# Feed-forward entries with in-place rows and direct sums, head norms rebuilt, forgetting scores as two passes of split operands

## The chip, the core and the metric

The kernel runs on one core of one Trainium2 chip. The metric is the device time of one execution in microseconds (us). A core has TensorE (matrix products, PE in the profile), VectorE (DVE), ScalarE (ACT), GpSimd (POOL) and SyncE (SP), whose queue here issues every transfer. Each engine works through its own list in order. Engines wait for one another by semaphores.

## What is computed

One layer of 1024 tokens, width 1024, in float32: two gated feed-forward blocks of inner width 2816 with a mixer and a cross attention to a memory of 256 rows between them. Each part has a norm ahead of it and one behind it. The mixer has eight heads of forgetting attention (64 wide) and four heads of gated linear attention (GLA). The parts that the change touches:

```python
# forgetting attention, for head h; c is the running sum of log_f
s = einsum('bhqd,bhkd->bhqk', qf[:, :, q0:L], kf[:, :, :L])       # qf holds q * 64 ** -0.5
s = s + c[:, :, q0:L, None] - c[:, :, None, :L]
p = softmax(where(mask, s, -inf));  o = einsum('bhqk,bhkd->bhqd', p, vf)
# norms of the heads, gate of GLA, output projection
o_fox = head_rms_norm(o, g_fox_out)
o_gla = head_rms_norm(gla_chunked(gq, gk, gv, log_a), g_gla_out) * silu(r)
y = concatenate([o_fox, o_gla]) @ w_out
# feed-forward
y = (silu(h @ w_gate) * (h @ w_up)) @ w_down
```

## The kernel before

Everything is static: each engine's list is written out in the code, and semaphores with constant counts order the engines.

*Products.* Most products are made of split operands: a high part (float32r, a rounded float32) and a low part (the remainder), three products each (hi hi, hi lo, lo hi). ScalarE makes the high part with a copy, VectorE the low part with a subtraction. Scores and a few others take float32 directly.

*Feed-forward, first half (`ff_1`).* Gate and up blocks of 256 columns are formed by a Strassen scheme with seven products P1, P2, P6, P5, P7, P3, P4 in that order. Their operands from x are B11, B21, T2, T1, T3, B22, T4. T1 and T2 are sums over tiles of tokens (`sum_x`), T3 and T4 are sums on top of T2 (`sum_x_late`). The operands from the weights are four groups: 0 and 3 come from the raw weights (`w_raw`), 1 and 2 from sums (`w_sums`). `high_x`, `low_x`, `high_w` and `low_w` split them. `fork_off` is a ScalarE copy of a PSUM bank that lets the next product reuse it: P7 waits for the second, P3 for the third. P4 waits for two block sums of VectorE. In the first block (m = 0) the products wait also for the tiles of x.

*An entry* is what leads to that first block. Eight tiles of 128 tokens are squared (ScalarE), get a root (GpSimd), become rows (`make_row`, VectorE), are turned by eight 128x128 transpositions (`turn`, TensorE, line 1248) into two PSUM banks and copied to `h_all` (`keep_h`). At f = 0 the rows pass through two buffers (`h_rows[0]`); the last two loads of x wait for earlier rows. The up weights (m = 1) are loaded in `ff_loads`, only after all T3 and T4 sums, since T2 lies in the buffer of those weights. The second entry (f = 1) runs inside the output loop of the cross attention, and behind it.

*Forgetting attention (`attend_fox`, lines 1375 to 1399).* Pairs of heads p = 0 to 3, for each 16 steps a: head a // 8, query block b = a % 8. Step a of TensorE is the scores of a (width 128 (b + 1)), the transpositions of the exponentials of a - 1, and the product with v of a - 2. Between them VectorE takes the row maximum and ScalarE the exponential. A score is one float32 product over 66 rows: 64 of q and k, one that holds c and one that holds ones; c comes to these rows by way of DRAM (`c_rows`, `load_c`). Behind step 15 the next pair's q and k are projected (`project`, lines 1316 to 1318), and both halves of k must be kept (`keep_q`) before the next scores. The projections' weights have three buffer pairs (`wr`), and `high_s(n)` waits for the projection n - 3. Sets are numbered: S_Q + 2p and the next are q and k of a pair, GQ to GQ+3 are those of GLA, GV its values, GR its gate, OUT the output weights.

*Behind it* TensorE transposes `k_flat` (`turn_k`, line 1428), which ScalarE copies once it has split GV and GV+1, then projects GQ+2 and GQ+3.

*Output projection.* For each tile i of 128 tokens: `gla_out` (four heads into bank 2), squares on ScalarE, sums on VectorE, root on GpSimd (L714), two scalings on VectorE (L1985, L1988), the gains and the gate on GpSimd (L720, L723), then `turn_o` (line 1506), high and low part (L1046, L1995), and 48 products (`out_tile`). Behind a tile `square1`, `root1` and `scale_y` make the new x (L780, L627, L1720, L1724).

## Time and profile before

| what | us |
|---|---|
| median of 3 runs | 2424.4 |
| lowest, highest | 2418.94, 2438.99 |
| the profiled execution: its time | 2420.73 |
| the profiled execution: its span | 2418.9 |
| TensorE busy in the span | 2282.0 |
| VectorE, ScalarE, GpSimd busy | 1090.1, 776.5, 477.2 |

The span is from the first to the last instruction. L1278 is line 1278 of the kernel. A row of the order of time gives the start, the duration, engine, line, operation, out<-in, the shapes and how many are merged; in brackets stands how long the engine was idle before it and what released it. The releaser is inferred: where the named one had long been done, it was another. "issue" means that nothing in the profile explains the idle time. The ends of products are modelled, so starts are the better measure. The granted clock is TensorE's, 1.00 for full speed.

### The profile page before, as it was taken

The numbers are of one execution on the slowest core, as the hardware profiler recorded it, in microseconds if no ns is written. First come the engines' busy times: TensorE is split into PE (matmuls) and PEld (weight loads), VectorE is DVE, ScalarE is ACT, GpSimd is POOL, SyncE is SP. The second block draws the span as 40 slices with busy tenths as digits, with TensorE's granted clock in tenths as the row PEclk, the third lists the DMA queues.
The fourth block names the chain that finished last, engine by engine and source line by source line (L and its number), as shares of the span: only waits on it lengthen the run. The fifth ranks groups of instructions, "written<-read, shape, count | busy, mean of one in ns | idle before, by whom it ended". The sixth has DMA issues, their size and how long they took to land.

```text
span 2418.9 us, 27006 instructions
## 1 busy us (share of the span) xinstructions
PE 2282.0 (94%) x10640; PEld 1856.6 (77%) x10640; DVE 1090.1 (45%) x1332; ACT 776.5 (32%) x1218; POOL 477.2 (20%) x455
## 2 busy tenths in 40 slices
PE   4899999999999999999999899989699999999997
PEld 3688888878877777778777687758588888878886
DVE  6444444464455244452234443234744444445446
ACT  5333333331123423331222243333533333332113
POOL 1344434300011000000123300001134434320003
PEclk8999999999999999999998899989799999999999
DMA  2222222253332000001221152023122222233323
GB/s 96 87 79 91 93 70 87 70 174 97 114 102 83 26 19 19 19 27 53 76 82 53 44 183 79 18 70 93 64 70 87 87 88 88 70 130 123 107 93 122
DMA packets 104958, 195.45 MB, mean 81 GB/s; under 512 B 6993, under 2 KB 72546, under 8 KB 102018
## 3 DMA queue, kind: packets, MB, share of 16 engines
q1 hardware_dynamic: 104834, 193.73, 24.4%
q8 instruction: 86, 1.41, 0.2%
q14 instruction: 38, 0.31, 0.0%
HBM read 153.80 MB, written 39.91 MB: 80 GB/s over the span
## 4 chain that ended last, share of the span: by engine, by line
issue 46%; PE 44%; POOL 4%; DVE 2%; POOLq 2%; ACT 1%; DMA 1%; DVEq 0%; SPq 0%; ACTq 0%
PE ps L1278 10%; PE ps L1279 10%; PE ps L1280 10%; PE ps L1296 3%; PE ps L1297 3%; PE ps L1298 3%; PE ps L1316 1%; PE ps L1318 1%; PE ps L1317 1%; POOL rs L627 1%; POOL rs L634 1%; POOL o_rms L714 1%; POOLq L721 1%; POOLq L633 0%; DMA w_raw<-in_w_ff_up 0%
## 5 line engine op out<-in xcount | busy, mean ns | idle before, releaser
L1278 PE MATMUL ps<-xc,wg 128*128 128x512 f32 x1232 | 484.4, 393 | 40.2 <-ACT fork L831 13.4
L1279 PE MATMUL ps<-xc,wg 128*128 128x512 f32 x1232 | 483.6, 392 | 0.0
L1280 PE MATMUL ps<-xc,wg 128*128 128x512 f32 x1232 | 482.9, 392 | 0.0
L1278 PEld LDWEIGHTS ps<-xc,wg 128*128 128x128 f32 x1232 | 234.0, 190 | 91.0 <-issue 37.6
L1296 PE MATMUL ps<-d_w,d_hid 128*128 128x512 f32 x704 | 276.1, 392 | 6.7 <-DVE y L1821 6.7
L1297 PE MATMUL ps<-d_w,d_hid 128*128 128x512 f32 x704 | 275.1, 391 | 0.0
L1298 PE MATMUL ps<-d_w,d_hid 128*128 128x512 f32 x704 | 275.0, 391 | 0.0
L1280 PEld LDWEIGHTS ps<-xc,wg 128*128 128x128 f32 x1232 | 233.8, 190 | 49.0
L1279 PEld LDWEIGHTS ps<-xc,wg 128*128 128x128 f32 x1232 | 233.9, 190 | 48.6
L1788 DVE TENSOR_TENSOR wg<-w_sums,wg 128x1024 fp32r<-128x1024 f32 x88 | 123.4, 1402 | 196.8 <-ACT wg L825 196.8
L1824 DVE TENSOR_TENSOR y<-y,ps 128x1024 f32<-128x1024 f32 x88 | 107.4, 1220 | 216.2 <-PE ps L1298 216.2
L1296 PEld LDWEIGHTS ps<-d_w,d_hid 128*128 128x128 f32 x704 | 133.0, 189 | 35.6 <-issue 7.5
L1788 DVE TENSOR_TENSOR wg<-w_raw,wg 128x1024 fp32r<-128x1024 f32 x88 | 129.4, 1471 | 55.8 <-ACT wg L825 55.8
L1298 PEld LDWEIGHTS ps<-d_w,d_hid 128*128 128x128 f32 x704 | 132.8, 189 | 27.8
L1297 PEld LDWEIGHTS ps<-d_w,d_hid 128*128 128x128 f32 x704 | 133.0, 189 | 27.5
L831 ACT ACTIVATE fork<-ps 128x512 f32<-128x512 f32 x132 | 78.7, 597 | 228.1 <-PE ps L1280 228.1
L654 POOL TENSOR_TENSOR hid<-hid,up_sum 128x512 f32<-128x512 f32 x66 | 89.2, 1352 | 265.0 <-DVE up_sum L1801 265.0
L825 ACT ACTIVATE wg<-w_sums 128x1024 fp32r<-128x1024 f32 x88 | 93.0, 1057 | 112.0 <-PE ps L1280 110.4
L625 POOL TENSOR_SCALAR ms<-ss 128x1 f32<-128x1 f32 x32 | 7.1, 223 | 572.4 <-ACT junk L780 572.4
L853 ACT ACTIVATE d_hid<-raw 128x1024 fp32r<-128x1024 f32 x44 | 46.5, 1057 | 220.1 <-PE ps L1298 134.4
L825 ACT ACTIVATE wg<-w_raw 128x1024 fp32r<-128x1024 f32 x88 | 74.3, 844 | 128.7 <-PE ps L1280 120.5
L641 POOL TENSOR_TENSOR w_sums<-w_raw 128x512 f32<-128x512 f32 x42 | 73.8, 1757 | 197.5 <-DVE wg L1788 145.2
(263 smaller groups left out, 3834.2 us busy)
## 6 DMA issues: line engine op xcount, KB each, us to landing
w_raw<-in_w_ff_gate SPq DMA_DIRECT2D x22, 1024.0 KB, 6.6
w_raw<-in_w_ff_up SPq DMA_DIRECT2D x22, 1024.0 KB, 5.2
hid_dram<-hid SPq DMA_DIRECT2D x22, 1024.0 KB, 4.6
raw<-hid_dram SPq DMA_DIRECT2D x44, 512.0 KB, 3.7
raw<-in_w_ff_down SPq DMA_DIRECT2D x44, 512.0 KB, 3.6
raw<-in_w_mix_in SPq DMA_DIRECT2D x24, 512.0 KB, 3.8
x_row<-x_dram SPq DMA_DIRECT2D x24, 512.0 KB, 4.1
x_dram<-x_ring SPq DMA_DIRECT2D x16, 512.0 KB, 5.0
```

The lines of the kernel that those rows point to most:

```text
L641: gp.tensor_tensor(s[1], r[:, 0:4, 1, :], r[:, 4:8, 1, :], ALU.add).then_inc(w_summed, 1)
L654: gp.tensor_tensor(blk, blk, up_sum[:, j, :], ALU.mult).then_inc(hid_done, 1)
L825: sc.activation(group_dst(g, 0), group_src(m, g), ACT.Copy).then_inc(w_hi_done, 1)
L831: sc.activation(fork[:, j, :], ps[:, 3 * (m % 2) + (0, 0, 2)[j], :], ACT.Copy).then_inc(forked, 1)
L1278: mm(acc, hi, x_hi, start=STARTS[q] and k == 0, stop=False, skip_group_check=True)
L1279: mm(acc, hi, x_lo, start=False, stop=False, skip_group_check=True)
L1280: last = mm(acc, lo, x_hi, start=False, stop=k == 3, skip_group_check=True)
L1296: mm(acc, a_hi, b_hi, start=c == 0, stop=False)
L1297: mm(acc, a_hi, b_lo, start=False, stop=False)
L1298: last = mm(acc, a_lo, b_hi, start=False, stop=c == GROUPS[f][gi] - 1)
L1788: ve.tensor_tensor(group_dst(g, 1), group_src(m, g), f32(group_dst(g, 0)), ALU.subtract).then_inc(w_lo_done, 1)
L1824: op = ve.tensor_tensor(y[:, i, :], y[:, i, :], two_banks(2 * UNIT_PAIR[u]), ALU.add)
```

## The change

1. *First entry.* Rows are made in place of x (`h_rows[0]` is `x_first`, which has eight buffers of its own), so that no load waits. Turned tiles use three pairs of banks. T1 is formed from PSUM directly (`sum_t1`), and T2 by `sum_t2`; for tiles 4 to 7 only the lower half is copied to `h_all`. T2 lies in the buffer of T4, which replaces it in place. The up weights are loaded right behind x. On ScalarE the second and third `fork_off` of the first block move ahead of the splits of the up weights, and on VectorE two block sums move forward.
2. *Second entry.* The same sums, and the up weights are loaded with the gate weights during the cross attention. `sum_t2` stands behind the loop.
3. *Scores.* q and k are kept as high and low parts. `qa` holds q's high part twice and `ka` k's high part above its low part (128 rows). `qb` holds q's low part and six rows for c, `kb` k's high part and six rows (70 rows). A score is two float32r products, at least 256 columns wide. c is split into three parts, which travel by DRAM, and the rows opposite hold ones or minus ones. Scores wait for the first half of k, at step 4 for the second half, at step 8 for the second head's `kb`.
4. *Weights of projections* have two buffer pairs, `high_s(n)` waits for projection n - 2, and the split of GQ+2 moves behind the attention.
5. *Head norms.* The gains are one column for each 128 rows of w_out (`head_gain`, eight small loads) and are multiplied into the output weights as these are split. The forgetting heads are normed in S during the products of GR. The GLA heads get root and gate in one VectorE operation a head. `turn_o` and the splits of its result are separate for the two halves, and the second low part stands behind `scale_y`.

```diff
-        wr = [[at_kb(f"wr{s}{a}", ((160, 164), (66, 84), (111, 75))[s][a], [P, KT, P], F32R) for a in range(2)]
-              for s in range(3)]
...
-                if i >= 6:
-                    sp.wait_ge(h_row_done, i - 5)
                 sp.dma_start(x_first[i][:, :], x[0][tile_of(i), :]).then_inc(x_in[i], 16)
+            load_weights(0, 1)
...
             def ff_1(f):
+                if f == 0:
+                    act.wait_ge(turned, 2 * NT)
                 high_w(f, 0, 2)
-                for q in (OP_T3, OP_B22, OP_T4):
+                for q in (OP_T3, OP_B22):
                     for j in range(4):
                         high_x(f, q, j)
+                fork_off(f, 0, 1)
+                high_w(f, 0, 3)
+                for j in range(4):
+                    high_x(f, OP_T4, j)
+                    if j == 1:
+                        fork_off(f, 0, 2)
                 for m in range(NM):
                     gate, nxt = m % 2 == 0, m + 1 < NM
                     if not gate:
                         silu(f, m // 2, 3)
-                    high_w(f, m, 3)
                     if m > 0:
+                        high_w(f, m, 3)
                         fork_off(f, m, 0)
                     if nxt:
...
                 elif n < S_GV:
-                    act.wait_ge(proj_done, event(n - 3, 1))
+                    act.wait_ge(proj_done, event(n - 2, 1))
...
+                if S_OUT <= n < S_MQ:
+                    act.wait_ge(head_gain_in, 16 * KT)
                 for dst, src in split_parts(n, 0):
-                    last = sc.activation(dst, src, ACT.Copy)
+                    if S_OUT <= n < S_MQ:
+                        last = sc.activation(dst, src, ACT.Copy, scale=head_gain[:, n - S_OUT:n - S_OUT + 1])
+                    else:
+                        last = sc.activation(dst, src, ACT.Copy)
                 last.then_inc(d_hi_done, 1)
...
-                dst, factor = ((q_head, FOX_D ** -0.5), (k_head, 1.0))[(n - S_Q) % 2]
-                sc.activation(dst[0][0:FOX_D, half(t)], ps[0:FOX_D, bank + t, :], ACT.Copy,
-                              scale=factor).then_inc(proj_act, 1)
+                c = half(t)
+                if (n - S_Q) % 2 == 0:
+                    parts = ((qa[0], 0, 0), (qa[0], FOX_D, 0), (qa[1], FOX_D, FOX_D))
+                else:
+                    parts = ((ka[0], 0, 0), (kb[0], 0, 0), (ka[1], FOX_D, FOX_D))
+                for dst, to, at in parts:
+                    op = sc.activation(dst[to:to + FOX_D, c], ps[at:at + FOX_D, bank + t, :], ACT.Copy,
+                                       scale=1.0 if (n - S_Q) % 2 else FOX_D ** -0.5)
+                op.then_inc(proj_act, 1)
...
-            high_s(S_GQ + 3)
-            for n in (S_GV, S_GV + 1):
+            for n in (S_GQ + 2, S_GQ + 3, S_GV, S_GV + 1):
...
-                    square_o(i + 1)
-                    high_o(i + 1)
+                    square_g(i + 1)
+                    high_o(i + 1, 0)
                 square1(2, i)
+                if i + 1 < NT:
+                    high_o(i + 1, 1)
                 if i > 0:
...
             def scores(p, a):
                 hh, b = divmod(a, 8)
+                if a in (0, 4):
+                    pe.wait_ge(proj_dve, event(S_Q + 2 * p + 1, a // 4))
+                if b == 0:
+                    pe.wait_ge(c_in[hh], 32 * p + 32)
+                if a == 8:
+                    pe.wait_ge(kb1_done, 2 * p + 2)
                 if a >= 2:
                     pe.wait_ge(exp_done, 16 * p + a - 1)
                 width = (b + 1) * P
-                q = q_head[hh][0:66, tile_of(b)]
                 for t in range((width + HT - 1) // HT):
                     w = min(HT, width - t * HT)
                     acc = ps[:, 2 * (a % 2) + t, :]
                     diagonal = (t + 1) * HT >= width
-                    mm(acc[:, 0:w], q, k_head[hh][0:66, t * HT:t * HT + w], start=True, stop=not diagonal)
+                    cols = slice(t * HT, t * HT + max(w, 2 * P))
+                    mm(acc[:, 0:max(w, 2 * P)], qa[hh][:, tile_of(b)], ka[hh][:, cols], start=True, stop=False)
+                    mm(acc[:, 0:max(w, 2 * P)], qb[hh][:, tile_of(b)], kb[hh][:, cols], start=False, stop=not diagonal)
                     if diagonal:
                         mm(acc[:, w - P:w], ident_b[:, :], neg_mask[:, :], start=False, stop=True).then_inc(score_done, 1)
...
+            def turn_o(i, b):
+                if b:
+                    pe.wait_ge(o_normed, i + 1)
+                    pe.wait_ge(att_kept, min(i + 2, NT))
+                else:
+                    pe.wait_ge(f_normed, i + 1)
+                wait(pe, o_t_lo, 2 * i - 1 + b)
+                src = o_tile[i % 2][:, HT:D] if b else S[:, i, 0:HT]
+                for k in range(4):
+                    last = nc.tensor.transpose(ps[:, 3 - 3 * b, tile_of(k)], src[:, tile_of(k)], ident[:, :])
+                last.then_inc(o_turned, 1)
...
+            def sum_t1(f, j):
+                dve.wait_ge(turned, 48 * f + 2 * (4 + j) + 1)
+                dve.wait_ge(h_all_done, kept(f, j))
+                ve.tensor_tensor(x_src(OP_T1, j), cols4(ps[:, turn_bank(3 * f, 4 + j), :]), x_src(OP_B11, j),
+                                 ALU.subtract).then_inc(x_t1, 1)
+
+            def sum_t2(f, j):
+                dve.wait_ge(h_all_done, kept(f, 4 + j))
...
                 dve.wait_ge(proj_done, event(n, t))
                 if n > S_Q + 1:
                     dve.wait_ge(score_done, 16 * ((n - S_Q) // 2))
-                if (n - S_Q) % 2:
-                    op = ve.tensor_copy(k_head[1][0:FOX_D, half(t)], ps[FOX_D:P, bank + t, :])
-                else:
-                    op = ve.tensor_scalar(q_head[1][0:FOX_D, half(t)], ps[FOX_D:P, bank + t, :], FOX_D ** -0.5, None, ALU.mult)
+                dve.wait_ge(proj_act, act_event(n, t))
+                c, lower, upper = half(t), slice(0, FOX_D), slice(FOX_D, P)
+                if (n - S_Q) % 2 == 0:
+                    ve.scalar_tensor_tensor(out=qb[0][lower, c], in0=ps[lower, bank + t, :], scalar=FOX_D ** -0.5,
+                                            in1=f32(qa[0][lower, c]), op0=ALU.mult, op1=ALU.subtract)
+                    ve.scalar_tensor_tensor(out=qb[1][lower, c], in0=ps[upper, bank + t, :], scalar=FOX_D ** -0.5,
+                                            in1=f32(qa[1][upper, c]), op0=ALU.mult, op1=ALU.subtract)
+                    op = ve.tensor_copy(qa[1][lower, c], f32(qa[1][upper, c]))
+                else:
+                    ve.tensor_tensor(ka[0][upper, c], ps[lower, bank + t, :], f32(ka[0][lower, c]), ALU.subtract)
+                    op = ve.tensor_tensor(ka[1][lower, c], ps[upper, bank + t, :], f32(ka[1][upper, c]), ALU.subtract)
                 op.then_inc(proj_dve, 1)
+
+            def keep_k1(p, t):
+                if p == 0:
+                    dve.wait_ge(b_done, 4)
+                    dve.wait_ge(suf_done, 4)
+                ve.tensor_copy(kb[1][0:FOX_D, half(t)], f32(ka[1][FOX_D:P, half(t)])).then_inc(kb1_done, 1)
...
+            def norm_g(i):
+                t = o_tile[i % 2]
                 dve.wait_ge(o_rms_done, i + 1)
                 dve.wait_ge(o_sum_done, i + 1)
...
+                dve.wait_ge(gr_kept, i + 1)
+                for h in range(4):
+                    c = slice(HT + P * h, HT + P * h + P)
+                    op = ve.scalar_tensor_tensor(out=t[:, c], in0=ps[:, 2, tile_of(h)], scalar=o_rms[:, i % 2, 8 + h:9 + h],
+                                                 in1=S[:, i, 1024 + P * h:1024 + P * h + P], op0=ALU.mult, op1=ALU.mult)
+                op.then_inc(o_normed, 1)
+
+            def low_o(i, b):
+                dve.wait_ge(o_t_hi, 2 * i + b + 1)
+                hi, lo = (t[:, 4 * b:4 * b + 4, :] for t in o_t)
+                ve.tensor_tensor(lo, cols4(ps[:, 3 - 3 * b, :]), f32(hi), ALU.subtract).then_inc(o_t_lo, 1)
...
-            ve.tensor_scalar(c_sb[1][:, :], c_sb[0][:, :], -1.0, None, ALU.mult).then_inc(c_done, 1)
+            for i in range(3):
+                wait(dve, c_split, 2 * i)
+                op = ve.tensor_copy(c_part[i][:, :], c_sb[:, :])
+                if i < 2:
+                    op.then_inc(c_split, 1)
+                    dve.wait_ge(c_split, 2 * i + 1)
+                    ve.tensor_tensor(c_sb[:, :], c_sb[:, :], f32(c_part[i][:, :]), ALU.subtract).then_inc(c_split, 1)
+                else:
+                    op.then_inc(c_done, 1)
             keep_q(S_Q + 1, 1, 0)
             keep_decay(1)
+            for t in range(2):
+                keep_k1(0, t)
...
+                if i + 1 < NT:
+                    sum_g(i + 1)
                 if i + 2 < NT:
                     keep_att(i + 2)
                     next_state(i + 2)
                 if i + 1 < NT:
-                    norm_o(i + 1)
-                    low_o(i + 1)
+                    norm_g(i + 1)
+                    low_o(i + 1, 0)
                 scale_y(2, i)
+                if i + 1 < NT:
+                    low_o(i + 1, 1)
                 if i > 0:
                     low_h(2, i - 1)
                 make_row(2, i)
```

The first place is ScalarE at the first block of the first feed-forward. wg is a weight split (wg_67 to wg_70 before and wg_66 to wg_69 with the change are the four groups), fork is `fork_off`, w_raw_72 before and w_raw_71 with the change are the up weights, xs_64 is T4, hid the gate. Before:

```order
L825 ACTIVATE wg_69<-w_sums 128x1024
L816 ACTIVATE xc<-xs_63 128x4x128 x4
L816 ACTIVATE xc<-h_all 128x4x128 x4
L816 ACTIVATE xc<-xs_64 128x4x128 x4
L825 ACTIVATE wg_70<-w_raw_71 128x512
L825 ACTIVATE wg_67<-w_raw_72 128x1024
L842 ACT_TABLE_LOAD
L842 ACTIVATE hid_73<-hid_73 128x512
L831 ACTIVATE fork<-ps 128x512 x2
```

With the change:

```order
L842 ACTIVATE wg_68<-w_sums 128x1024
L833 ACTIVATE xc<-xs_63 128x4x128 x4
L833 ACTIVATE xc<-h_all 128x4x128 x4
L848 ACTIVATE fork<-ps 128x512
L842 ACTIVATE wg_69<-w_raw_70 128x512
L833 ACTIVATE xc<-xs_64 128x4x128 x2
L848 ACTIVATE fork<-ps 128x512
L833 ACTIVATE xc<-xs_64 128x4x128 x2
L842 ACTIVATE wg_66<-w_raw_71 128x1024
```

The last row of before holds the second and the third fork copy, three rows behind the first split of the up weights; now both stand ahead of that split, the third between the splits of T4.

The second place is ScalarE between the last step of the attention and the copies of k_flat. wr and gvw are splits of weights, raw_87 and raw_88 (86 and 87 in the change) the two raw tiles. Before:

```order
L1020 ACTIVATE probs_t_147<-ps 128x384
L1020 ACTIVATE probs_t_148<-ps 128x512
L946 ACTIVATE wr_137<-raw_87 128x1024
L946 ACTIVATE gvw_170<-raw_88 128x512
L946 ACTIVATE gvw_171<-raw_88 128x512
L946 ACTIVATE gvw_172<-raw_87 128x512
L946 ACTIVATE gvw_173<-raw_87 128x512
L1026 ACTIVATE k_flat_168<-ps 128x512 x2
```

With the change:

```order
L1053 ACTIVATE probs_t_146<-ps 128x384
L1053 ACTIVATE probs_t_147<-ps 128x512
L975 ACTIVATE wr_134<-raw_87 128x1024
L975 ACTIVATE wr_132<-raw_86 128x1024
L975 ACTIVATE gvw_171<-raw_87 128x512
L975 ACTIVATE gvw_172<-raw_87 128x512
L975 ACTIVATE gvw_173<-raw_86 128x512
L975 ACTIVATE gvw_174<-raw_86 128x512
L1059 ACTIVATE k_flat_169<-ps 128x512 x2
```

One more split of wr (GQ+2) stands there, and the two share two buffer pairs instead of three.

The third place is TensorE at the first steps of the attention: k_head and q_head, and ka, qa, kb, qb are the operands of scores. Before:

```order
L1375 MATMUL ps<-k_head_143,q_head_141 128x128
L1377 MATMUL ps<-neg_mask,ident_b 128x128
L1375 MATMUL ps<-k_head_143,q_head_141 128x256
L1377 MATMUL ps<-neg_mask,ident_b 128x128
L1388 MATMUL ps<-ident,probs_145 128x128
L1375 MATMUL ps<-k_head_143,q_head_141 128x384
```

With the change:

```order
L1430 MATMUL ps<-ka_138,qa_136 128x256
L1431 MATMUL ps<-kb_142,qb_140 128x256
L1433 MATMUL ps<-neg_mask,ident_b 128x128
L1430 MATMUL ps<-ka_138,qa_136 128x256
L1431 MATMUL ps<-kb_142,qb_140 128x256
L1433 MATMUL ps<-neg_mask,ident_b 128x128
L1444 MATMUL ps<-ident,probs_144 128x128
L1430 MATMUL ps<-ka_138,qa_136 128x384
```

Each score product became two, and 128 columns became 256.

## Rows read from the trace of the kernel before

**Rows 1.** The page: busy time, share of the span and instructions of TensorE.

```profile
PE 2282.0 (94%) x10640; PEld 1856.6 (77%) x10640; DVE 1090.1 (45%) x1332; ACT 776.5 (32%) x1218; POOL 477.2 (20%) x455
```

**Rows 2.** TensorE's waits: who waited for whom, total, times, longest (us).

```profile
PE ps L1278 <- ACT fork L831: 13.4, 1, 13.4
...
PE ps L1506 <- POOL o_tile L723: 9.1, 4, 2.6
```

**Rows 3.** Table of stretches: length, busy (count) by engine, granted clock, DMA share, GB/s.

```profile
73.00:83.03 10.03, 10.03 (x36) 8.13 (x37) 3.93 (x4) 3.65 (x5) 3.81 (x4) 0.81 0.00 0
840.60:1100.47 259.87, 253.99 (x1504) 201.02 (x1505) 126.37 (x286) 83.73 (x189) 0.00 (x0) 1.00 0.08 23
905.42:943.04 37.62, 37.13 (x242) 28.12 (x243) 25.80 (x58) 16.30 (x39) 0.00 (x0) 1.00 0.11 29
1228.29:1393.34 165.05, 150.11 (x744) 117.61 (x745) 73.77 (x111) 37.64 (x68) 58.32 (x69) 0.87 0.18 58
1286.34:1293.66 7.32, 7.32 (x65) 5.40 (x63) 3.26 (x4) 3.17 (x6) 0.74 (x2) 1.00 0.01 2
1293.66:1304.84 11.18, 11.18 (x50) 8.93 (x48) 7.03 (x14) 2.16 (x4) 4.04 (x6) 1.00 0.31 94
1430.00:1440.00 10.00, 10.00 (x85) 10.00 (x85) 3.98 (x4) 4.21 (x4) 0.00 (x0) 1.00 0.55 177
1748.72:1758.85 10.13, 10.12 (x37) 8.19 (x37) 3.93 (x4) 3.66 (x5) 3.82 (x4) 0.80 0.00 0
```

**Rows 4.** Order of time, both entries.

```profile
23.77 1.22 DVE L1788 TENSOR_TENSOR wg<-w_raw,wg 128x1024 fp32r<-128x1024 f32 x1 [0.17 <-ACT wg L825]
...
53.54 0.77 PE L1278 MATMUL ps<-xc,wg 128*128 128x512 f32 x1 [5.55 <-DVE xc L1782]
...
57.46 2.49 DVE L1782 TENSOR_TENSOR xc<-xs,xc 128x512 fp32r<-128x512 f32 x4
...
69.41 1.06 ACT L825 ACTIVATE wg<-w_raw 128x1024 fp32r<-128x1024 f32 x1 [4.07 <-DMA w_raw<-in_w_ff_up]
...
72.32 1.06 ACT L831 ACTIVATE fork<-ps 128x512 f32<-128x512 f32 x2
...
73.00 0.76 PE L1278 MATMUL ps<-xc,wg 128*128 128x512 f32 x1 [10.88 <-issue]
...
1727.39 0.76 PE L1278 MATMUL ps<-xc,wg 128*128 128x512 f32 x1 [6.30 <-DVE xc L1782]
```

**Rows 5.** Groups by line and shape: union of busy us, mean ns, idle before.

```profile
L1375 PE MATMUL ps<-k_head,q_head 66*128 66x512 f32 x96 | 50.0, 615 | 0.0
...
L963 ACT ACTIVATE k_head<-ps 64x512 f32<-64x512 f32 x8 | 4.7, 590 | 46.3 <-PE ps L1318 46.3
...
L1889 DVE COPY k_head<-ps 64x512 f32<-64x512 f32 x8 | 5.5, 693 | 34.0 <-PE ps L1318 34.0
...
L714 POOL TENSOR_TENSOR o_rms<-o_mean,minus_half 128x12 f32<-128x12 f32 x8 | 18.2, 2278 | 1.2 <-issue 0.2
```

**Rows 6.** Order of time at the start of the second pair, TensorE.

```profile
905.42 0.46 PE L1375 MATMUL ps<-k_head,q_head 66*128 66x128 f32 x2 [0.83 <-DVE k_head L1889]
...
906.81 0.33 PE L1388 MATMUL ps<-ident,probs 128*128 128x128 f32 x1 [0.33 <-ACT probs L1013]
```

**Rows 7.** Order of time, c and its way through DRAM.

```profile
833.30 0.68 DVE L2086 TENSOR_SCALAR c_sb<-c_sb 8x1024 f32<-8x1024 f32 x1
...
836.46 0.21 SPq L525 DMA_DIRECT2D q_head<-c_rows  x1
```

**Rows 8.** Order of time behind the attention, and the page's DMA issues (us to landing).

```profile
1100.47 1.09 PE L1428 MATMUL ps<-ident,k_flat 128*128 128x128 f32 x8 [1.41 <-ACT k_flat L1026]
...
raw<-in_w_mix_in SPq DMA_DIRECT2D x24, 512.0 KB, 3.8
```

**Rows 9.** Order of time behind an output tile.

```profile
1289.46 1.03 ACT L780 ACTIVATE junk<-ps 128x1024 bf16<-128x1024 f32 x1
...
1292.97 1.23 DVE L1724 TENSOR_TENSOR x_ring<-x_ring,x_row 128x1024 f32<-128x1024 f32 x1
```

340 lines of the change are left out of this document (192 added, 148 removed).

## The prediction

> **What bounds the kernel now.** I read the page's first part, then TensorE's waits, then a table of stretches, then the order of time at the stretches that stand out. TensorE is busy 2282.0 us of a span of 2418.9 [rows 1], so nothing matters that does not shorten TensorE's own work, a wait of TensorE, or a stretch at half clock. The waits name two places in each feed-forward entry and one in the output projection: 13.4 us (second entry) and 10.9 (first) ahead of the fifth product of a first gate block, and 9.1 us for o_tile [rows 2, 4]. The table adds the price: the output projection takes 165.05 us for 150.11 of work at a granted clock of 0.87, of which 1.00 is 2.4 GHz and 0.5 is 1.2 GHz; the forgetting attention takes 259.87 at full clock with next to no idle time [rows 3]. So there the change must remove work, and elsewhere waits.
>
> **Step 1, the first entry.** What holds TensorE at 73.00 is not the tiles of x. ScalarE's activation that frees the bank (fork, 72.32) stands behind a weight split (69.41) that waits for the load of the up weights, which the SyncE queue sends only after the T4 sums [rows 4]. The profile calls that wait "issue"; the order of ScalarE shows its cause. With the change those weights are loaded with x, and ScalarE runs fork before that split. The next limit is VectorE, and I lay its list end to end. An operation of 512 elements costs 0.60 (four in 2.49 [rows 4]), one of 1024 twice that, and each hand-over to ScalarE and back 0.7. The low part of the first weights ends at 25.0 today [rows 4] and at 25.6 with a fifth row ahead of it. From there to the last low part of T2 there are three rows, eight sums, four weight sums, seven low parts, one weight part and four hand-overs: 3.8 + 5.2 + 2.4 + 4.2 + 1.2 + 2.8, so the third product starts at about 45.1 instead of 53.54. It and the fourth take 8.2 as they do today. Behind them VectorE needs 0.6 + 2.4 + 1.2 + 2.4 for T3 (51.7, so the fifth need not wait: 53.3), 4.8 more for B22 (the sixth at 56.5, ending at 59.2), and 4.3 more for the last operand and two block sums (60.8). That product takes 2.7, and the up block starts at 63.5 instead of 83.03 [rows 3]: **-19.5**. One stretch at half clock (ten us for 36 products, granted clock 0.81 [rows 3]) goes with it, which is within the sum.
>
> **Step 2, the second entry.** Two of three T2 sums move from inside the output loop, where VectorE idled, behind it: the product at 1727.39 [rows 4] comes 1.8 later. The rest goes as above: third pair done at 1737.2, T3 ready 1737.6, B22 1742.4, last operand 1746.7, up block at 1749.4 instead of 1758.85: **-9.4**. Here TensorE waits twice for VectorE, 2.3 and 1.6 us.
>
> **Step 3, the scores themselves.** A float32 score product is two passes in the trace, 96 of 512 columns take 50.0 us of union [rows 5], and start to start one full product takes 0.89. The change makes two split products of it. Products of that kind run at 0.229 each for 512 columns in the output projection (11.0 us for 48), and the memory keys, mixed from 256-column products, at 0.12 (85 in 10 us) [rows 3]. Per head, the widths 128 to 1024, with the floor of 256, come to 4.4 us where the eight tiles take 8.0 now: 3.6 x 8 = 29 us of TensorE's work. Not all is kept. In a pair of 37.62 us VectorE is busy 25.80 [rows 3]; TensorE's own work falls to about 30, so TensorE will wait for row maxima and exponentials: laid out step by step, about 0.8 us more a pair than it does today.
>
> **Step 4, what the pairs pay at their starts.** Today one activation (590 ns) and one copy (693) of 64x512 keep a projected half [rows 5], side by side, and the first transposition comes at 906.81, 2.2 after the projection's last product [rows 6]. With the change VectorE subtracts ScalarE's result from PSUM, so they stand in series: three activations 1.65, two subtractions 1.3, two copies of keys 0.7, and behind them on VectorE's queue the first row maximum. The first transposition comes 4.5 after the projection: 2.25 later. A pair then ends 4.7 earlier: 7.2 of products less and 0.5 of small waits (as in [rows 6]) gone, 2.25 of start and 0.8 of waits more. In the first pair the running sum c is split in three: today 0.68 for a negation [rows 7], with the change five operations of 8x1024, 0.68 for a copy and 1.2 for a subtraction, 4.6 in all, behind two more subtractions (1.3) and a longer wait for ScalarE (0.7). Its way through DRAM takes 2.5 from the end of the negation (833.98) to the next issue (836.46) [rows 7] and about as much back. So scores start at 845.2 instead of 840.60, 4.6 later. VectorE's copies of SBUF data cost 0.68 per 1024 elements [rows 7] and its two-operand subtractions 1.2. The Trainium skill, VectorE: DVE Perf Modes, section on the perf-mode tier table, has the same rule, twice the rate for a float32 copy in SBUF and none for two operands; if casts fell out of it, this chain would be 1.6 longer. Sum at full clock: -2.4 for the first pair, -4.7 x 3 = -14.1, together -16.5. Each start then leaves TensorE nearly idle for 4 to 5 us. After the waits of 10.9 and 13.4 us the clock is granted at 0.81 and 0.80 over the next ten [rows 3], a loss of about 1.8 each. I charge 5 for the four starts: **-11.5**.
>
> **Step 5, behind the attention.** With two weight sets for three, set GQ+3 may be split only when the last projection has ended (1099.1 [rows 8]), not one projection sooner. In ScalarE's order stand then: this split 1.06, VectorE's low part 1.2, the load of GV+1 into the same raw tile 3.8 [rows 8], its split 1.15, two k_flat activations 1.1 (the kind of [rows 5]). The transpositions of k_flat stand ahead of the next projections on TensorE, at 1100.47 now [rows 8], at 1107.4 then: 6.9, and 2 of half clock: **+8.9**. So the whole attention gives only 2.6, and of 29 us of removed work most comes back as waits.
>
> **Step 6, the output projection.** Three GpSimd operations of a tile leave the path, and the square root for twelve columns (2278 ns [rows 5]) shrinks to four. A tile is 11.0 of products [rows 3]; between two stand 7.32 of small products (one less, 6.3, in the first) [rows 3], which nothing shortens. The wait that may replace the old one: the low part of the second half now stands behind the scaling of the tile before. From the start of the square (1289.46) to the end of the addition (1292.97 + 1.23) it is 4.74 [rows 9]; with 1.15 ahead (the first half's activation goes first) and 0.7 behind, products can resume 6.6 after the last tile. That hides under 7.32 five tiles deep, and shows at the first (0.3) and the last two (1.7 and 4.6). So 8 x 11.0 + 6.6 + 4 x 7.32 + 2 x 6.6 = 137.1 instead of 165.05, less 0.7 for a fox square ahead of the last weight split, less 2 of half clock: **-25.4**. The gains move into the weights' splits at no cost: same counts, hidden by the products of GR.
>
> **Sum.** -19.5 - 9.4 - 2.6 - 25.4 = -57. The profiled execution took 2420.7 us (span 2418.9), 3.7 below the median of 2424.4 and within the runs shown: 2364.
>
> **The rivals.** *The attention keeps its gain:* starts cost half and the clock stays up: about 16 more, 2348. For it: today's short waits at the starts leave the clock at 1.00 [rows 3]. Against: the series on two engines is in the code. *VectorE sets the attention's pace:* steps 6 to 9 of each pair carry a split of 1.2 on top of 2.3 of its own work where TensorE has 2.6 to 3.0. If all three pairs run at its pace, step 3 loses 16: 2380. *The head norms do not get shorter,* because every tile still ends in the chain of two engines: the stretch stays near 165, 2389. Against it: 7.3 covers 6.6, but only by 0.7. *Slower:* every start of a pair drops the clock and the small products never bring it back before the pair ends. A pair's 30 us of TensorE work then take up to 55, and four such pairs lose 100: 2464. It decides from 57 us lost, three pairs in four. Against it: the loop of today, the same small products, holds 1.00 over 259.87 us [rows 3]. The Trainium skill, TensorE: Matmul & The Clock Gate, section on oscillation, tells of a kernel whose short bursts between waits each start at half clock; by that rule every start would pay, and here it would be 2 for each, the sum above, not the whole pair.
>
> **Chances.** Forecast 0.57, attention keeps 0.14, VectorE's pace 0.13, norms no shorter 0.11, slower 0.03, something else 0.02. The range 2346 to 2386 takes in the first three and leaves out the last. A measurement of this kernel tells about 1% from no change, so faster means under 2400: 0.94; same 0.04; slower 0.02.
>
> **What would show it.** Right: the third product of the first entry near 45 us, the up block near 63.5 and 1749.4 less what went before; a pair 4.7 shorter with an idle TensorE of 4 us at its start; k_flat 8 us behind the last projection; output tiles 18.3 apart at clock 1.00. Wrong: a new wait for xc in the first block of over 3 us, a score loop whose waits for maxima exceed 3 us a pair, or tiles more than 20 apart.

## The result, and the profile after

The change makes the kernel 0.5% faster: 2412.66 us as the median of 20 runs (2407.1 to 2422.55) against 2425.03 of 20 runs before, a ratio of 0.9947 with a 95% interval of 0.9928 to 0.9967. The forecast was 2364. The profiled execution took 2410.01 (span 2408.3), 10.7 less than the one of before; 46 of the 57 us are missing.

Where the two traces part, by the lead of the changed kernel at the same instruction of TensorE:

| place (before, after) | lead | the piece gave | forecast |
|---|---|---|---|
| up block of the first entry (83.03, 68.43) | 14.6 | 14.6 | 19.5 |
| a projection ahead of the attention (805.54, 793.24) | 12.3 | -2.3 | 0 |
| first scores (840.60, 832.66) | 7.9 | -4.4 | -4.6 |
| transpositions of k_flat (1100.47, 1094.99) | 5.5 | -2.4 | 9.2 |
| first output tile (1228.29, 1224.95) | 3.3 | -2.2 | -2.7 |
| behind the last output tile (1393.34, 1389.72) | 3.6 | 0.3 | 26.1 |
| first product of the second entry (1710.39, 1704.21) | 6.2 | 2.6 | 0 |
| up block of the second entry (1758.85, 1749.22) | 9.6 | 3.4 | 9.4 |
| end (2418.9, 2408.3) | 10.6 | 1.0 | 0 |

The forecast's 16.1 from the first scores on, less its 6.9 for k_flat, is the 9.2 of the fourth row; its 2 of half clock and its 0.7 for a square stand in the fifth. Three pieces lie over parts that the change hardly touches (-2.3, 2.6 and 1.0). There the idle time is the same to 1 us, and TensorE's time at half clock is not: 5.2 us before and 12.6 after in the first, 17.1 and 10.2 in the second, 16.8 and 10.2 in the last.

TensorE's busy time fell by 15.6 us from [rows 1], from the page:

```profile
PE 2266.4 (94%) x10640; PEld 1862.5 (77%) x10640; DVE 1117.5 (46%) x1392; ACT 791.0 (33%) x1242; POOL 475.5 (20%) x447
```

TensorE's waits after (total, times, longest). The fork of [rows 2] is gone with its 13.4 us, and so are the 10.9 of the first entry and the 9.1 for o_tile. Their successors are new names:

```profile
PE ps L1327 <- DVE xc L1845: 21.1, 4, 8.9
...
PE ps L1444 <- ACT probs L1046: 14.6, 10, 4.1
PE ps L1521 <- DVE o_t L2095: 9.3, 5, 2.7
...
PE ps L1481 <- ACT k_flat L1059: 8.3, 1, 8.3
PE ps L1327 <- DVE hid L1864: 7.7, 2, 3.8
...
PE ps L1365 <- DVE o_t L2095: 6.2, 2, 4.6
PE ps L1430 <- DMA kb<-c_rows: 5.4, 1, 5.4
```

They are the third and the sixth product of the entries (L1327 waiting for xc: 8.9 and 1.6 us in the first, 8.7 and 1.9 in the second, 21.1 in all, where the kernel before had 11.9 for the third products), the last product of each first block (L1327 waiting for hid: 7.7), the first transposition of a pair (L1444: 14.6), the small products of the next output tile (L1521: 9.3) and the output products themselves (L1365 for o_t: 6.2), k_flat (8.3) and c (5.4).

The table of stretches after, which answers [rows 3] (length, busy by engine, granted clock, DMA share, GB/s):

```profile
64.23:68.43 4.20, 4.20 (x12) 3.38 (x13) 4.20 (x4) 2.14 (x3) 1.29 (x1) 0.65 0.00 0
832.66:1094.99 262.33, 239.23 (x1505) 207.70 (x1505) 138.62 (x310) 97.06 (x213) 0.00 (x0) 0.94 0.09 24
898.01:913.16 15.15, 15.05 (x96) 13.05 (x97) 11.56 (x24) 8.04 (x17) 0.00 (x0) 0.82 0.13 35
913.16:930.99 17.83, 17.47 (x142) 15.87 (x142) 13.56 (x33) 7.66 (x21) 0.00 (x0) 1.00 0.13 34
1224.95:1389.50 164.55, 149.11 (x744) 117.06 (x745) 69.13 (x120) 34.55 (x62) 23.85 (x49) 0.87 0.18 56
```

First the last product of the first gate block, then the whole attention, the first and the second head of its second pair (the first begins at 898.01, 4.9 behind the pair's first score), and the output projection. That last one is the plainest miss: 164.55 us at a clock of 0.87, where [rows 3] has 165.05 at 0.87.

### The profile page after: what moved, and what is told of

It reads as the page before. It is cut to its first block and busy times, and to the rows that moved or that the text cites. A ratio compares the mean times of both kernels' runs of the same rounds, so it can differ in the third digit from the quotient of the medians.

```text
span 2408.3 us, 27129 instructions
## 1 busy us (share of the span) xinstructions
PE 2266.4 (94%) x10640; PEld 1862.5 (77%) x10640; DVE 1117.5 (46%) x1392; ACT 791.0 (33%) x1242; POOL 475.5 (20%) x447
## 3 DMA queue, kind: packets, MB, share of 16 engines
q8 instruction: 86, 1.41, 0.2%
## 5 line engine op out<-in xcount | busy, mean ns | idle before, releaser
L1327 PE MATMUL ps<-xc,wg 128*128 128x512 f32 x1232 | 485.2, 394 | 29.1 <-DVE xc L1845 21.1
L1327 PEld LDWEIGHTS ps<-xc,wg 128*128 128x128 f32 x1232 | 234.2, 190 | 80.9 <-issue 22.2
```

The lines of the kernel that those rows point to most:

```text
L1327: mm(acc, hi, x_hi, start=STARTS[q] and k == 0, stop=False, skip_group_check=True)
```

## The experiments

All of them start from the changed kernel. Medians come from 4 to 6 runs each; the run with one product less and the two repeated profiles are single runs. "Less than the changed kernel" compares medians (its own is 2412.66). The ratio to before is taken on the same chip and is the fairer measure; the changed kernel's is 0.9947 (0.9928 to 0.9967). "A first head" is the time from the first transposition of a pair (step 0) to that of step 7, "a second head" from step 8 to step 14, both read in the order of time.

**The low part ahead of the scaling.** In the changed kernel's output tile, VectorE's rows and the one that waits for them:

```profile
1311.32 1.28 DVE L1779 SCALAR_TENSOR_TENSOR x_ring<-ps,rs,gb 128x1024 f32<-128x1024 f32 x1 [1.29 <-POOL rs L636]
...
1312.71 1.23 DVE L1783 TENSOR_TENSOR x_ring<-x_ring,x_row 128x1024 f32<-128x1024 f32 x1
1313.85 0.68 DVE L2095 TENSOR_TENSOR o_t<-ps,o_t 128x512 fp32r<-128x512 f32 x1
...
1314.68 0.57 PE L1521 MATMUL ps<-S 64*128 64x128 f32 x3 [1.65 <-DVE o_t L2095]
```

The last row is the first product of the next tile's GLA work. It writes the bank that the low part at 1313.85 reads, and that low part stands behind two rows of `scale_y`. Only 4.9 us of small products (1308.1 to 1313.0) lie ahead of that wait; the forecast hid the chain under all 7.32 of them.

```diff
                     low_o(i + 1, 0)
+                    low_o(i + 1, 1)
                 scale_y(2, i)
-                if i + 1 < NT:
-                    low_o(i + 1, 1)
```

> The changed kernel, with one thing moved: on VectorE the low part of the second half (low_o(i + 1, 1)) stands ahead of scale_y(2, i) instead of behind it. Theory 1: the output projection did not get shorter because the first small products of the next tile (L1521) reuse the bank that this low part reads, and the low part stood behind the scaling: 2.7 us at the first tile, 1.65 at four more, 1.6 and 4.6 at the last two, and each wait leaves TensorE at half clock. Then the idle time of the stretch falls from 16.6 to about 5, the stretch of eight tiles from 164.6 to between 142 and 153, and the whole by 12 to 22 us against the changed kernel. Rival: the scaling, 0.7 later, delays the next rows and the next tile just as much: the stretch stays within 3 us of 164.6.

Measured: 2392.73 us, 20 less than the changed kernel (18 by the two ratios); ratio to before 0.9874 (0.9852 to 0.9896). The stretch of the eight tiles:

```profile
1227.60:1365.43 137.83, 134.52 (x744) 106.74 (x745) 69.03 (x120) 34.57 (x62) 23.85 (x49) 0.97 0.22 69
```

It is 137.8 us at a clock of 0.97, better than expected. The order of time shows the low part ahead of the scaling and the product behind the transpositions without a wait:

```profile
1300.52 0.69 DVE L2095 TENSOR_TENSOR o_t<-ps,o_t 128x512 fp32r<-128x512 f32 x1 [1.27 <-ACT o_t L1085]
...
1301.13 1.27 DVE L1779 SCALAR_TENSOR_TENSOR x_ring<-ps,rs,gb 128x1024 f32<-128x1024 f32 x1
...
1302.18 0.71 PE L1521 MATMUL ps<-S 64*128 64x128 f32 x4
```

Theory 1 holds, its rival does not: the scaling, later by one row of 0.69, delays nobody but the last two tiles (waits for x_ring, 3.2 us in all). Idle time fell by 12.3 us (16.6 to 4.3, sums of the gaps), and TensorE's busy time for the same 744 products by 14.6 (149.11 to 134.52): behind the second tile the clock stays at 1.00 to the end of the stretch.

**GpSimd's sums held back.** Both engines' rows in the changed kernel's first entry:

```profile
49.95 2.49 DVE L1845 TENSOR_TENSOR xc<-xs,xc 128x512 fp32r<-128x512 f32 x4
50.10 8.91 POOL L652 TENSOR_TENSOR w_sums<-w_raw 128x512 f32<-128x512 f32 x1 [4.18 <-DVE wg L1851]
...
58.37 5.16 DVE L1845 TENSOR_TENSOR xc<-xs,xc 128x512 fp32r<-128x512 f32 x4
...
58.97 1.73 POOL L654 TENSOR_TENSOR w_sums<-w_sums,w_raw 128x512 f32<-128x512 f32 x1
...
64.23 0.76 PE L1327 MATMUL ps<-xc,wg 128*128 128x512 f32 x1 [3.84 <-DVE hid L1864]
```

Four low parts take 2.49 us at 49.95 and 5.16 at 58.37, with the same shapes (one by one 1.19, 1.77, 1.75 and 0.68). GpSimd's sum of 128x512 takes 8.91 while VectorE works without a gap, though the mean of this sum in the kernel before was 1550 ns (L643 there). In the kernel before, the up weights came only at 69.41 [rows 4], when VectorE's list was done.

```diff
                 wait(pool, w_lo_done, 4 * (n - 1) + 2)
+                if m == 1:
+                    pool.wait_ge(xc_lo_done, X_COUNT[f][OP_T4, 3])
```

> The changed kernel, with one wait added: GpSimd's sums of the first up weights of each feed-forward (sum_weights at m = 1) start only when VectorE has written the last low part of T4. Theory 2: these sums, possible early because the up weights are there early, collide with VectorE's operations on SBUF: 1.78 us instead of 0.68 for three of the low parts and 8.9 us for one sum of GpSimd. Then all low parts in the entry take 0.68, the last product of the first gate block (P4) starts at 61 to 61.5 instead of 64.23, the up block at 64.0 to 65.5 instead of 68.43, the same again in the second entry: 6 to 9 us in all. Rival: the slow operations have another cause and stay at 1.78; then the up block waits for its sums, which are late now, and the time is 2 to 6 us longer than that of the changed kernel.

Measured: 2404.09 us, 8.6 less than the changed kernel by the medians, but only 3 by the ratios: 0.9935 (0.9914 to 0.9956) overlaps 0.9947 (0.9928 to 0.9967), so the whole time alone does not show the gain. The order of time shows it where it arises:

```profile
57.14 2.48 DVE L1847 TENSOR_TENSOR xc<-xs,xc 128x512 fp32r<-128x512 f32 x4
...
59.80 1.27 POOL L652 TENSOR_TENSOR w_sums<-w_raw 128x512 f32<-128x512 f32 x1 [27.05 <-DVE xc L1847]
...
60.33 0.47 PE L1329 MATMUL ps<-xc,wg 128*128 128x512 f32 x1 [1.18 <-DVE hid L1866]
61.03 2.27 POOL L654 TENSOR_TENSOR w_sums<-w_raw 128x512 f32<-128x512 f32 x1
```

Four low parts in 2.48, GpSimd's first sum in 1.27 and the one that took 8.91 (L652 there, L654 here) in 2.27, the last product at 60.33 (forecast: 60.8), the up block at 63.15 (forecast: 63.5). In the second entry the up block starts 39.5 us behind the entry's first product, instead of 45.0 with the change and 48.5 before: 9.0 where the forecast said 9.4. In each up block a wait of 1.1 for a fork is new (2.2 in all), the price of sums that come late. In all the entries give 5.3 and 5.5, less 2.2, about the 8.6 of the medians. So VectorE and GpSimd do stand in each other's way here. The Trainium skill, SBUF — State Buffer, section on two separate sides, says that a VectorE operation with two inputs in SBUF and a GpSimd operation that reads SBUF exclude each other for a whole instruction; both rows above agree (8.91 for the one that found no gap, up to 1.1 more for a VectorE operation that ran beside a sum of 1.6 to 1.7). That the lock is the mechanism, and not something else that the two share, no run here tells.

**The second half of k behind the first exponentials.** The series at the start of a pair in the changed kernel:

```profile
893.26 0.59 ACT L997 ACTIVATE ka<-ps 64x512 fp32r<-64x512 f32 x1 [3.76 <-PE ps L1367]
...
894.35 0.59 ACT L997 ACTIVATE ka<-ps 64x512 fp32r<-64x512 f32 x1
895.07 0.68 DVE L1970 TENSOR_TENSOR ka<-ps,ka 64x512 fp32r<-64x512 f32 x1 [4.04 <-ACT ka L997]
...
896.38 0.75 DVE L1978 CAST kb<-ka 64x512 fp32r<-64x512 f32 x2
897.17 0.62 DVE L1999 TENSOR_REDUCE neg_max<-ps 128x1 f32<-128x128 f32 x2
897.50 0.37 ACT L1046 ACTIVATE probs<-ps,neg_max 128x128 f32<-128x128 f32 x1 [2.56 <-DVE neg_max L1999]
...
898.01 0.47 PE L1444 MATMUL ps<-ident,probs 128*128 128x128 f32 x1 [4.10 <-ACT probs L1046]
```

ScalarE keeps three pieces (893.26 to 894.94), VectorE subtracts twice and copies twice, and only then comes the first maximum, its exponential, and the transposition that waited 4.10 us.

```diff
# attend_fox, on ScalarE and on VectorE, at the end of step a
+                    if a == 1 and p > 0:
+                        keep_q(S_Q + 2 * p + 1, 1, 2)    # VectorE: and keep_k1(p, 1)
...
```

> The changed kernel, with the order of two engines changed in pairs 1 to 3 of the attention: ScalarE's and VectorE's keeping of the second half of k (three activations, two subtractions, one copy) stands behind the first two exponentials and row maxima instead of ahead of them. Theory 3: the idle 4.1 us at the start of each of these pairs is the series of ScalarE and VectorE in front of the first maximum, and the half clock of the 6 us behind it is its result. Then the idle time falls to about 1.3 a pair, the clock stays up or is down for less, and the whole is 9 to 15 us shorter than the changed kernel. Rival: the same series is then waited for at step 4, which needs the second half of k: the wait of 3 to 4 us moves there and less than 4 us are gained in all.

Measured: 2413.14 us (ratio 0.996, 0.9947 to 0.9973): nothing gained. The rival was right in substance:

```profile
896.85 0.33 PE L1447 MATMUL ps<-ident,probs 128*128 128x128 f32 x1 [0.51 <-ACT probs L1046]
...
898.37 0.59 ACT L997 ACTIVATE ka<-ps 64x512 fp32r<-64x512 f32 x1
...
899.09 0.68 DVE L1973 TENSOR_TENSOR ka<-ps,ka 64x512 fp32r<-64x512 f32 x1 [1.59 <-ACT ka L997]
...
900.85 0.56 DVE L2002 TENSOR_REDUCE neg_max<-ps 128x1 f32<-128x384 f32 x1
...
902.17 0.55 PE L1447 MATMUL ps<-ident,probs 128*128 128x128 f32 x3 [3.35 <-ACT probs L1046]
```

The first transposition comes after 0.51 us, and the transpositions of step 2 wait 3.35: the maximum of step 2 (900.85) stands behind the same three operations on VectorE, which wait for the same three on ScalarE. Step 2 waits, not step 4 as the rival said, since it is the queue that counts and not the operand.

**The same, with the series taken apart.**

```diff
# TensorE, behind attend_fox(p)
+                    for k in range(KT):           # the second half of k
+                        if k == 5:
+                            scores(p + 1, 0)
+                            scores(p + 1, 1)
...
# VectorE, end of step a: step 2 low part of ka[0], step 3 low part of ka[1],
#                         steps 4 and 5 the copies for the second head
+                    if p > 0 and a in (2, 3):
+                        keep_k_part(p, a - 2)
+                    if p > 0 and a in (4, 5):
+                        keep_k1(p, a - 4)
```

> The changed kernel with the starts of pairs 1 to 3 rebuilt: TensorE issues the first two scores of the next pair before the last three eighths of the projection of k's second half, so that their maxima and exponentials lie beside it; ScalarE keeps that half behind the first two exponentials, VectorE in two steps behind the maxima of steps 2 and 3, and the copies for the second head stand behind steps 4 and 5. Theory 3, mended after the run before: what is lost at a start is one series over two engines, and it goes only if no part of it stands between a maximum and its exponential. Then the first transposition follows the projection at once, at most 2 us in all are waited for in the first eight steps instead of 4.5, and the three pairs give 3 x 2.5 of wait and up to 3 x 2.7 of half clock: 8 to 15 us less than the changed kernel. Rival: step 4 or 5 waits for the kept half for over 3 us, as in the run before, and the gain is under 4.

Measured: 2399.58 us, 13.1 less than the changed kernel (12.6 by the ratios); ratio to before 0.9895 (0.9858 to 0.9932). A pair, and its first head:

```profile
890.39:950.86 60.47, 57.82 (x378) 49.91 (x377) 34.86 (x78) 24.72 (x54) 0.00 (x0) 1.00 0.07 19
893.28:909.17 15.89, 13.61 (x100) 11.62 (x99) 14.37 (x29) 9.89 (x20) 0.00 (x0) 1.00 0.13 33
```

A pair takes 60.47 us at full clock where it took 64.82 before (905.42 to 970.24) and 64.12 with the change. Waits of 0.71, 0.48 and 0.99 remain in a first head, 2.2 in all, and the clock stays at 1.00. Theory 3, mended, holds: that is 4.35 a pair against the kernel before, which the forecast (4.7 at full clock) had for the change itself.

**One product of each score left out.** Is it TensorE's work that sets the pace between the starts?

> The changed kernel with the first of the two products of each score (qa with ka) left out, so that the scores are not those of the reference; only its time is of use. Theory 5: outside the starts of the pairs TensorE's own work sets the pace of the attention. One pass of a pair is 2 x 4864 columns, 4.35 us at the 0.229 us for 512 columns of the output projection, so a pair falls from 64.1 to about 60 and the second head of a pair (from its first score to the projection of q, 17.8 us) to about 15.7. Rival, VectorE's pace (row maxima, copies and splits, the same here): a second head stays over 17.

Measured: 2420.07 us in one run, with 96 products fewer: 7 more than the median of the changed kernel, and inside its range (2407.1 to 2422.55). The four first heads:

```profile
833.67:853.68 20.01, 19.99 (x89) 17.68 (x89) 13.11 (x26) 8.92 (x19) 0.00 (x0) 0.50 0.10 27
902.47:916.98 14.51, 13.70 (x88) 11.75 (x89) 12.08 (x25) 8.51 (x19) 0.00 (x0) 0.81 0.14 36
964.22:984.24 20.02, 20.00 (x89) 17.68 (x89) 13.06 (x25) 8.78 (x19) 0.00 (x0) 0.50 0.10 27
1032.62:1052.64 20.02, 19.99 (x89) 17.68 (x89) 13.16 (x25) 8.76 (x19) 0.00 (x0) 0.50 0.10 27
```

Three of them ran wholly at half clock (0.50) and took 20.0 us; the one at 0.81 took 14.5. A second head, at full clock, took 11.4 instead of 12.6: 1.2 less where the forecast's price for one pass over those six steps is 1.9 (4352 columns at 0.229 for 512). Each second head now has a wait of 0.60 for an exponential, where the changed kernel has one of 0.36. By the measure of the expectation, from the first score of a second head to the projection, it took 16.4 behind the one first head at 0.81, between the 15.7 of the theory and the 17 of the rival; the other three (17.7 to 18.1) began at half clock. So neither theory is right alone: TensorE's work mostly sets the pace of a second head in the changed kernel, and 1.2 us further down the other two engines do. The products saved did not shorten this execution, because of the half clock in three of four first heads. Whether the missing products caused that, one run does not show: the next run has all its products, and its first heads took as long (74.8 us in all, 74.6 here).

**The copies of k_flat first.**

```diff
# ScalarE
-            for n in (S_GQ + 2, S_GQ + 3, S_GV, S_GV + 1):
-                high_s(n)
-            for t in range(2):
-                keep_k(0, t)
+            high_s(S_GQ + 2)
+            for t in range(2):
+                keep_k(0, t)
+            for n in (S_GQ + 3, S_GV, S_GV + 1):
+                high_s(n)
# VectorE: decay_k(0, t) ahead of low_s(S_GQ + 3) and low_s(S_GV)
```

> The changed kernel, with the copies of k_flat on ScalarE and the operation of VectorE that they follow (decay_k(0, t)) moved ahead of the splits of GQ + 3, GV and GV + 1. Theory 4: the 8.3 us ahead of the transpositions of k_flat are the splits and the load that stand before the copies on ScalarE, as the forecast had it. Then the transpositions start about 2.8 us behind the last projection, at 1089.4 instead of 1094.99, and with less half clock the whole gains 5 to 8 us. Rival: the splits and loads, now later, are waited for by the projections or the values of GLA, and less than 2 us are gained.

Measured: 2410.8 us (2402.25 to 2412.59), 1.9 less than the changed kernel where 5 to 8 were expected, and not told from it by the ratio, 0.9941 (0.9919 to 0.9963). The wait did go:

```profile
PE ps L1482 <- ACT k_flat L1059: 1.4, 1, 1.4
```

from 8.3 to 1.4. But the transpositions started at 1099.18 instead of 1094.99, because the pairs ahead of them had become longer, with the same instructions. Three first heads of this run:

```profile
833.19:853.65 20.46, 20.32 (x99) 17.88 (x100) 12.35 (x26) 8.58 (x19) 0.00 (x0) 0.60 0.10 26
902.30:922.35 20.05, 19.91 (x99) 17.48 (x100) 12.09 (x25) 8.42 (x19) 0.00 (x0) 0.62 0.10 27
1037.92:1053.95 16.03, 15.63 (x100) 13.61 (x100) 12.14 (x25) 8.62 (x19) 0.00 (x0) 0.81 0.13 34
```

At clocks of 0.60 and 0.62 a first head takes 20 us, at 0.81 it takes 16; the four together took 12 us more than in the changed kernel's first profile (14.98, 15.54, 15.90, 16.26). The runs with the low part moved and with GpSimd's sums held back leave the attention as it is, and their first heads lie within 0.11 of those four. Two more profiles ask whether that belongs to the kernel. The changed kernel again:

> The changed kernel itself, profiled once more. Question: is the time at half clock behind the start of a pair a property of the kernel (6.8 us at each of four starts in the first profile) or of the execution? If of the kernel, the first heads of the four pairs take 15.0, 15.5, 15.9 and 16.3 us again, within 0.2. If of the execution, at least one takes 18 or more, and the whole is 2 us or more longer for each such head. Its twenty times, 2407 to 2412 and 2417 to 2422, speak for the second.

Measured: 2411.1 us, first heads of 15.86, 16.06, 14.62 and 20.00. The shortest and the longest:

```profile
962.69:977.31 14.62, 14.49 (x99) 12.59 (x100) 11.98 (x25) 8.48 (x19) 0.00 (x0) 0.88 0.14 38
1025.89:1045.89 20.00, 19.86 (x100) 17.43 (x100) 12.19 (x25) 8.42 (x19) 0.00 (x0) 0.62 0.10 27
```

The one at 0.88, the other at 0.62. So one head passed 18, as expected if the length is the execution's; the whole came out 1.1 longer than in the first profile, not 2, since the third head was 1.3 shorter. And the kernel with the copies moved again:

> The changed kernel with the copies of k_flat moved, profiled once more: in its first profile the first heads took 20.5, 20.1, 18.3 and 16.0 us, at half clock for up to 20.5 us. If the length is one of the execution, at least two of them come out 2 us or more different, and the time follows: 2402 where all are near 16, 2412 where they are near 20. If it is one of the kernel, they repeat within 0.3.

Measured: 2408.39 us, first heads of 14.67, 20.05, 18.30 and 16.04: the first one 5.8 shorter than in its first profile (20.46), the others the same, and the time 4.2 shorter. One head moved where two were expected, so neither answer came out whole: the half clock behind a start is in part the execution's, 14.6 to 20.5 us for one and the same list of instructions, and three heads repeated, so the kernel has a share in it that these runs don't separate.

**All four repairs.**

> The changed kernel with four repairs at once: the low part ahead of the scaling in the output projection (20 us by its own run), GpSimd's first sums held back in both entries (8.6), the copies of k_flat first (its wait of 8.3 fell to 1.4, the median by 1.9), and the starts of pairs as in the run beside this one (8 to 15 if theory 3 holds). If the parts add up: 2412.7 less 20, 8.6, 5 and 8 to 15, or 2364 to 2371. If a drop of the clock at one place is only moved to another, it stays above 2378.

Measured: 2356.0 us (2353.92 to 2359.71, 6 runs), ratio to before 0.9716 (0.9683 to 0.9748): the fastest version here, 2.8% under the kernel before and 57 us under the changed one. It lies below what was expected of the sum. The page's first row and the attention from the first scores to k_flat:

```profile
PE 2238.2 (95%) x10640; PEld 1839.0 (78%) x10640; DVE 1111.9 (47%) x1392; ACT 791.3 (34%) x1242; POOL 462.1 (20%) x447
```

```profile
830.23:1073.38 243.15, 233.30 (x1505) 201.21 (x1505) 136.20 (x305) 94.43 (x208) 0.00 (x0) 0.99 0.08 21
```

243.15 us instead of 262.33, and TensorE's busy time is 28 us lower, most of it half clock that is no longer there.

**All but the copies of k_flat.**

> The kernel with the four repairs, less one: the copies of k_flat stand behind the splits again. Where the starts of pairs drop the clock, the move of these copies was worth 1.9 us of the median, though it took 6.9 us of idle time away. Theory 4: the rest was hidden by the clock, which in that run's profile was at half for 58 us of the attention instead of 27. Without those drops the move shows whole: this kernel is 7 to 10 us slower than the one with all four (2356.0), so 2363 to 2366. Rival: the move is worth little by itself, and this stays below 2360.

Measured: 2367.01 us (2363.45 to 2369.17); ratio to before 0.9779 (0.9761 to 0.9796). The move that gave 1.9 alone gives 11.0 in this company by the medians (15 by the two ratios, each against the kernel before on its own chip), more than the 7 to 10 expected. Of that 6.9 is the wait; behind it the next ten us hold 38 products at a clock of 0.75 without the move, and 48 at 1.00 with it:

```profile
1078.23:1088.23 10.00, 10.00 (x38) 8.42 (x39) 2.37 (x4) 2.13 (x4) 0.00 (x0) 0.75 0.19 54
```

```profile
1073.38:1083.38 10.00, 10.00 (x48) 8.44 (x49) 5.26 (x8) 4.24 (x7) 0.00 (x0) 1.00 0.41 113
```

## Why the prediction was wrong

The direction was right; the size and the range were not, and the measured 0.5% lies where the forecast had put a chance of 0.04. Its sums hold but for small slips that decide nothing: step 6 adds up to 25.25 and not 25.4 (165.05 less 137.1, 0.7 and 2), and the first wait of step 2 to 2.1 and not 2.3. By its steps:

*Step 1, first entry: half right.* Up to the fifth product the list of VectorE held to 0.4 us: the third product at 44.94 (45.1), the fifth at 52.94 (53.3), the sixth at 57.39 (56.5). Then the last came at 64.23 instead of 60.8 and took 4.2 instead of 2.7 at half clock. The term that failed is "4.3 more for the last operand and two block sums": it priced VectorE's operations as before, though the change brings the up weights early and so lets GpSimd's sums run beside them. With those held back the forecast's own numbers came out, 60.33 and 63.15. The kernel before had the shared cost in no row of the entry, but it had the reason: GpSimd's sums started only when the up weights came. The forecast asked what the early load frees and not what it sets going.

*Step 2, second entry: the same term.* 3.4 instead of 9.4, and 9.0 in the run with GpSimd held back. A smaller part of it was mis-sized too: the third product came 2.7 later in relation, not 1.8.

*Step 3, the scores: mis-sized.* A second head fell from 15.12 to 12.62 us, by 2.50, where 4224 columns at 0.89 for 512 (7.34) less 4352 x 2 at 0.229 (3.89) promised 3.45, less 0.4 for waits. The price of 0.229 is that of a row of equal products. Here it holds for all but the first product of a step, behind the 64-column products with v, which takes 0.31:

```profile
925.22 0.47 PE L1430 MATMUL ps<-ka,qa 128*128 128x512 f32 x1
925.53 0.39 PE L1431 MATMUL ps<-kb,qb 70*128 70x512 f32 x1
```

Six steps come to 4.47 instead of 3.89. With the 0.5 of small waits that did not go (one of 0.36 stands in every pair) a pair at full clock saved 5.2 (twice 2.50, and 0.18 between the heads), not 6.9: 6.9 in all four.

*Step 4, the starts: the series right, its price wrong.* From the projection to the first transposition it took 4.8 (forecast 4.5), and the first pair's scores were 4.4 late (4.6). What failed is the charge for the clock, 5 us for four starts. A first head should have saved as much as a second, 2.5; it saved 1.1, 0.6, 0.2 and -0.15, so the four lost 1.4, 1.9, 2.3 and 2.65, 8.3 in all, in this profile, and 12 more in the profile where the half clock lasted longest. With 6.9 for the pace, 3.3 for the clock and 0.9 for the series, 11.1 of the 11.6 us that the fourth row of the table misses have a name. The Trainium skill, TensorE: Matmul & The Clock Gate, section on oscillation, says that short bursts between waits each start cold. The trace agrees (clock 0.82 over the first head, 1.00 over the second), and "2 for each", which the forecast worked out beside that rule and did not use, is the measured mean. Its rival of a whole pair at half clock did not happen; a first head wholly at 0.50 did, three times in the run with one product less.

*Step 5, k_flat: right.* 8.3 us of wait against 1.41 before is 6.9, to the tenth.

*Step 6, the output projection: wrong, and the largest piece.* The step that failed is "products can resume 6.6 after the last tile. That hides under 7.32". The 6.6 was good (1308.08 to 1314.68); the cover was not, since 2.4 of the 7.32 are products that write the bank of that very low part and so stand behind the wait. The cover was 4.9 and showed 1.65 at four tiles, 2.68 at the first, 1.56 and 4.61 at the last two. The idle time of the stretch did not fall (15.4 before, 16.6 after, sums of the gaps), and its clock stayed at 0.87. One row moved on VectorE gives the forecast stretch: 137.8 against 137.1.

*The rivals.* "The norms no shorter" had 0.11 and this price (+25), with the right doubt (7.3 covers 6.6 only by 0.7) but not the reason. "Slower" had its condition right, every start of a pair dropped the clock, and its price wrong: 8.3 us lost here, not 100. VectorE's pace did not come true in the attention, where a second head waits 0.36 for another engine, but it set the pace of the entries, as steps 1 and 2 had it, with dearer operations. "The attention keeps its gain" did not come true either (262.33 us, 259.87 before). They were treated as one at a time, and parts of two came true together.

## What to carry to other kernels

When a chain is said to hide under other work, list which instructions of that work can run before it: those that touch its buffer stand behind it, and cover nothing. When a load or a wait is taken away, ask what else it held back, on every engine, and price it where it now runs. A wait of TensorE ahead of small products can bring half clock behind it (12.3 us of idle time and 14.6 of slower products went together in the output projection here), so a repair that ends it can be worth more than its row among the waits, and one such repair may show its worth only beside the others.

## What the runs showed of the hardware

- The half clock behind a wait of 4.1 to 5.4 us varies between executions of one list of instructions: a first head took 14.6 to 20.5 us, the clock over it 0.88 to 0.60.
- With 96 products taken out, three of four first heads ran at 0.50 throughout, lower than any first head of the other profiles (0.60), and the kernel took 2420.07 us. It is one run, and the cause is not shown.
- Three waits under 1 us in a first head (0.71, 0.48, 0.99) and one of 0.37 in the second left the clock at 1.00 over the pair.
- A float32 sum of 128x512 on GpSimd took 8.91 us beside VectorE's unbroken list of operations in SBUF; the same sum took 2.27 where it came behind the list. Two of VectorE's low parts took 1.77 and 1.75 beside GpSimd's sums instead of 0.68.
- A product of 512 columns of the split scores takes 0.31 us behind 64-column products and 0.23 to 0.24 behind one of its kind; one of 256 columns takes 0.12.
